# Differential heads joined ahead of one transpose and value product; latent heads scored in pairs

## What is computed

```
s = einsum('bqhmd,bkhmd->bhmqk', q, k) * scale + bias      # m = 0, 1: two score maps per head
p = softmax(s)
w = p[:, :, 0] - lam * p[:, :, 1]
o = einsum('bhqk,bkhd->bqhd', w, v)                        # one v for both maps
o = rms_norm(o, subln_g) * (1 - lam_init)
```

## Time and profile before

| | |
|---|---|
| median of 3 runs | 1736.49 us (1736.48 to 1736.52) |
| the profiled execution's own time | 1736.73 us |
| its span, first to last instruction | 1734.9 us |
| TensorE busy | 1584.0 us, 91% |
| VectorE, ScalarE, GpSimd busy | 938.1, 621.0, 218.0 us |
| mean granted TensorE clock | 0.96 of full |

### The profile page before, as it was taken

The page is one execution under the profiler, slowest core; times in us unless marked ns, Lnnn a source line. Parts: engine busy times, 40 slices in busy tenths (PEclk is TensorE's granted clock), DMA queues, the critical chain, the costliest instruction groups (busy, mean ns, idle before and its releaser), DMA issues.

```text
span 1734.9 us, 27116 instructions
## 1 busy us (share of the span) xinstructions
PE 1584.0 (91%) x10485; PEld 1216.5 (70%) x10485; DVE 938.1 (54%) x1543; ACT 621.0 (36%) x961; POOL 218.0 (13%) x241
## 2 busy tenths in 40 slices
PE   9999999777666677899999999999999999999998
PEld 6788985333223323688888888888888888888886
DVE  5675543111101111577786667777777767577767
ACT  5465441100010010433453653334433444553342
POOL 0232110000000000100015231000110114511000
PEclk9999999988889968999999999999999999999999
DMA  9515488999999999965545055533755445065501
GB/s 396 194 69 162 178 329 359 426 426 426 425 426 426 426 426 427 385 244 188 195 162 197 31 200 202 194 119 134 300 188 196 174 166 195 25 230 195 193 37 49
DMA packets 61100, 421.47 MB, mean 243 GB/s; under 512 B 7024, under 2 KB 16080, under 8 KB 17360
## 3 DMA queue, kind: packets, MB, share of 16 engines
q1 hardware_dynamic: 59280, 409.13, 60.0%
q10 hardware_dynamic: 1728, 11.03, 1.7%
HBM read 419.08 MB, written 1.05 MB: 242 GB/s over the span
## 4 chain that ended last, share of the span: by engine, by line
PE 69%; DMA 16%; SPq 6%; DVE 5%; ACT 2%; issue 2%; POOL 1%; DVEq 0%; ACTq 0%
PE bank L1168 17%; PE bank L1211 12%; DMA ring<-in_we 11%; PE bank L1170 9%; PE bank L2208 7%; SPq L2057 6%; PE bank L2137 5%; DMA more<-in_we 3%; PE bank L2372 2%; PE bank L2234 2%; PE bank L1551 2%; PE bank L2353 2%; PE bank L689 2%; DMA ring<-in_wf 2%; PE bank L1198 1%
## 5 line engine op out<-in xcount | busy, mean ns | idle before, releaser
L1168 PE MATMUL bank<-xhl,whu 128*128 128x512 f32 x1280 | 451.8, 396 | 0.0
L1170 PE MATMUL bank<-xhl,wlu 128*128 128x256 f32 x1280 | 357.5, 279 | 0.0
L1168 PEld LDWEIGHTS bank<-xhl,whu 128*128 128x128 f32 x1280 | 240.3, 188 | 57.8
L1170 PEld LDWEIGHTS bank<-xhl,wlu 128*128 128x128 f32 x1280 | 241.1, 188 | 3.3
L985 DVE TENSOR_TENSOR wlu<-ring,whu 128x2048 fp32r<-128x2048 f32 x84 | 192.5, 2292 | 43.8 <-ACT whu L980 43.8
L980 ACT ACTIVATE whu<-ring 128x2048 fp32r (+1 forms) x88 | 167.2, 1902 | 3.5 <-DMA ring<-in_wf 3.5
L985 DVE TENSOR_TENSOR wld<-ring,whd 128x1024 fp32r<-128x1024 f32 x80 | 98.6, 1233 | 113.3 <-ACT whd L980 113.3
L689 PE MATMUL bank<-ring,xg 128*32 128x256 f32 x1424 | 105.4, 436 | 38.1 <-DMA ring<-in_we 38.1
L980 ACT ACTIVATE whd<-ring 128x1024 fp32r (+1 forms) x80 | 84.8, 1060 | 128.5 <-PE bank L1211 128.5
L1278 ACT ACTIVATE sg<-sg 128x256 f32<-128x256 f32 x80 | 33.5, 418 | 265.8 <-DVE sg L1357 265.8
L2208 PE MATMUL bank<-ring_r,xTh 128*128 128x512 f32 x384 | 109.8, 397 | 4.6 <-DVE ring_r L520 2.5
(11 more groups left out here) (370 smaller groups left out, 2761.5 us busy)
## 6 DMA issues: line engine op xcount, KB each, us to landing
ring<-in_we SPq DMA_DIRECT2D x141, 1024.0 KB, 26.8
ring<-in_wf SPq DMA_DIRECT2D x88, 1536.0 KB, 6.5
ring<-in_w SPq DMA_DIRECT2D x52, 1024.0 KB, 5.1
more<-in_we SPq DMA_DIRECT2D x51, 1024.0 KB, 25.8
ring<-in_w SPq DMA_DIRECT2D x32, 256.0 KB, 3.7
ln<-in_ln ACTq DMA_DIRECT2D x6, 1024.0 KB, 6.0
bias<-in_bias ACTq DMA_DIRECT2D x2, 2048.0 KB, 9.4
bias<-in_bias SPq DMA_DIRECT2D x1, 2048.0 KB, 20.4
```

Of the source, the lines that this page charges most:

```text
L1168: pe.matmul(into[:].rearrange("p (a s) -> p a s", a=2), whu[p][:, cols], xhl[:, :, k], start=(k == 0), stop=False, skip_group_check=True)
L1170: ins = pe.matmul(into[:, 0:S], wlu[p][:, cols], xh[:, k], start=False, stop=(k == KD - 1), skip_group_check=True)
```

## The change

- The two score maps of a differential head are joined on VectorE as soon as both exponentials are there (`mix`): the second map, times minus lambda and the ratio of the two sums, is added to the first. The pair then has one transpose, one copy, one value product (`values2`: 16 in place of 20) and one output. The output of the value product before stands behind the join. The probabilities have a fourth buffer (`lg_d`, over the differential queries and keys).
- TensorE transposes a pair behind the scores of its second unit, and takes the values in the next unit.
- Latent queries and keys are laid out as the 64 plain columns of all heads and then the 32 rotated ones. Their transposes are three groups in place of four. A latent head's scores are two products (64 rows and 32 rows), and the heads are scored in pairs, the products of the two heads alternating (`AHEAD2`).
- Scores of units 14 and 15 no longer wait for the latent transposes (`QK_READY`). ScalarE's scaling of cat block 1 moves behind unit 18.
- In the first feed-forward pass ScalarE makes the high part of tile 1 behind the four casts of the activations. GpSimd makes half of its low part and VectorE the other half, and TensorE's `up(1, 1)` waits for these two alone.

```diff
+        lg_d = proj2[:, 0, D0:D0 + NT * S].rearrange("p (t s) -> p t s", t=NT)
...
-            q, _ = head_rows(qkT2, block2(10 + h), 0, BQ)
-            _, k = head_rows(qkT2, block2(14 + h), 0, BQ)
-            units2.append(Unit([q], [k], [vm[:, t, h, :] for t in range(NT)], 1.0,
+            qs = [head_rows(qkT2, block2(b), r, n)[0] for b, r, n in ((10 + h // 2, 64 * (h % 2), 64), (14, 32 * h, 32))]
+            ks = [head_rows(qkT2, block2(b), r, n)[1] for b, r, n in ((12 + h // 2, 64 * (h % 2), 64), (15, 32 * h, 32))]
+            units2.append(Unit(qs, ks, [vm[:, t, h, :] for t in range(NT)], 1.0,
...
         AHEAD2 = {0: (2, 3), 1: (4, 5), 3: (6, 7), 5: (8, 9), 7: (10, 11), 9: (12, 13), 11: (14, 15),
-                  **{u: (u + 4,) for u in range(12, 16)}}
+                  13: (16, 17), 15: (18, 19)}
...
+        values2 = [(n, n + 1) if unit.half == 0 else (n,) for n, unit in enumerate(units2) if unit.half != 1]
+        value_of = {n: v for v, heads in enumerate(values2) for n in heads}
+        PAIRS2 = sum(len(heads) == 2 for heads in values2)
+        VALUES2 = len(values2)
+        lg_buffers = [lg2[:, 0], lg2[:, 1], lg2_c[:], lg_d]
+        lg_at = [0, 1, 2, 0, *((n - 3) % 4 for n in range(4, UNITS2))]
+        lg_last = [max((m for m in range(n) if lg_at[m] == lg_at[n]), default=None) for n in range(UNITS2)]
+        lg_free = [0 if m is None else value_of[m] + 1 for m in lg_last]
...
+        def pool_second(pool, g, between=None, columns=range(0, 2 * D, 512)):
...
             pool.wait_ge(wh_ok, g * FFN_W + 2)
-            ffn_low_pieces(pool, 1, 1, pre_ok, between)
+            ffn_low_pieces(pool, 1, 1, pre_ok, between, columns)
...
+            def up(t, p, ready=None):
+                pe.wait_ge(*(ready or (wl_ok, t * 2 + (g * FFN_W + FFN_W + 1))))
...
-            up(1, 1)
+            up(1, 1, (pre_ok, 2) if g == 0 else None)
...
             if g == 0:
-                act_second(act, 0)
                 for j in range(4):
                     act.wait_ge(t_ps, tb + (j + 1))
                     act.activation(xh[:, 2 * j:2 * j + 2].rearrange("p k s -> p (k s)"), bank[4 + j][:], ACT.Copy)\
                        .then_inc(xh_ok, 1)
+                act_second(act, 0)
                 act_high_down(act, 0)
...
+            if g == 0:
+                dve.wait_ge(wh_ok, 2)
+                ffn_low_pieces(dve, 1, 1, pre_ok, columns=SECOND_HALF)
             dve.wait_ge(wh_ok, g * FFN_W + 3)
             ffn_low(dve, 0, 0, True, wl_ok)
-            dve.wait_ge(pre_ok, g + 1)
+            dve.wait_ge(pre_ok, g + 2)
             dve.memset(small[:, 234:235], 0.0).then_inc(wl_ok, 1)
...
-        QK_READY = {4: 7, 8: 10, 12: 11, 14: 15, 16: 15}
+        QK_READY = {4: 7, 8: 10, 12: 11, 16: 15}
...
-                    for k in range(2):
-                        ins = pe.matmul(bank[b][:, 0:BH * BQ], cT[:, k, tok(i)], slot[s][:, k * BH * BQ:(k + 1) * BH * BQ],
-                                        start=(k == 0), stop=(k == 1))
+                    for into, columns in ((slice(0, NOPE), slice(0, 64)), (slice(NOPE, BH * BQ), slice(64, BQ))):
+                        for k in range(2):
+                            w = slot[s][:, k * BH * BQ:(k + 1) * BH * BQ].rearrange("p (h d) -> p h d", h=BH)
+                            ins = pe.matmul(bank[b][:, into].rearrange("p (h d) -> p h d", h=BH), cT[:, k, tok(i)], w[:, :, columns],
+                                            start=(k == 0), stop=(k == 1))
                     ins.then_inc(mla_ps, 1)
...
-                    if 8 <= u < 12:
+                    if 8 <= u < 11:
                         j = u - 8
                         pe.wait_ge(t_out, tb + 11 + j)
                         for b in range(2):
                             for i in range(NT):
-                                ins = pe.transpose(bank[7][0:BQ, b * S + i * P:b * S + (i + 1) * P],
-                                                   (qm, km)[j % 2][:, i, 2 * (j // 2) + b], ident[:])
-                        ins.then_inc(t_ps, 1)
+                                part = (qm[:, i, b * P:(b + 1) * P], km[:, i, b * P:(b + 1) * P], (qm, km)[b][:, i, NOPE:])[j]
+                                ins = pe.transpose(bank[7][:, b * S + i * P:b * S + (i + 1) * P], part, ident[:])
+                        ins.then_inc(t_ps, (1, 1, 2)[j])
...
             for i in range(NT):
-                for unit in units:
-                    for b in range(len(unit.q)):
+                for b in range(len(units[0].q)):
+                    for unit in units:
                         ins = pe.matmul(bank[unit.bank][:, i * S:(i + 1) * S], unit.q[b][i], unit.k[b],
                                         start=(b == 0), stop=(b == len(unit.q) - 1))
-                    if i == NT - 1:
-                        ins.then_inc(sc_ps, 1)
+                        if i == NT - 1 and b == len(unit.q) - 1:
+                            ins.then_inc(sc_ps, 1)
...
+            def probs_T(v):
+                u = values2[v][0]
+                pe.wait_ge(pt_ok, v0 + v - 1)
+                if units[u].half is None:
+                    pe.wait_ge(ex_ok, n0 + u + 1)
+                else:
+                    pe.wait_ge(mix_ok, l * PAIRS2 + sum(len(heads) == 2 for heads in values2[:v + 1]))
+                lg = lg_buffers[lg_at[u]]
                 for t in range(NT):
                     for i in range(NT):
-                        ins = pe.transpose(bank[2 + u % 2][:, t * S + i * P:t * S + (i + 1) * P],
-                                           lg_ring[u % 3][:, i, t * P:(t + 1) * P], ident[:])
+                        ins = pe.transpose(bank[2 + v % 2][:, t * S + i * P:t * S + (i + 1) * P], lg[:, i, t * P:(t + 1) * P], ident[:])
                 ins.then_inc(pt_ps, 1)
+            def values(v):
+                unit = units[values2[v][0]]
+                pe.wait_ge(o_ok, v0 + v - 1)
+                pe.wait_ge(pt_ok, v0 + v + 1)
+                for i in range(NT):
+                    for t in range(NT):
+                        ins = pe.matmul(bank[4 + v % 2][:, i * unit.dv:(i + 1) * unit.dv], pT_at[:, v % 2, t, tok(i)], unit.v[t],
+                                        start=(t == 0), stop=(t == NT - 1))
+                ins.then_inc(pv_ps, 1)
...
+            for u, unit in enumerate(units):
+                v = value_of[u]
+                if unit.half is None:
+                    probs_T(v)
+                    if v >= 1:
+                        values(v - 1)
                 if u >= 1:
-                    values(u - 1)
                     between(u)
                     if u in AHEAD2:
                         scores(AHEAD2[u])
+                if unit.half == 0:
+                    values(v - 1)
+                elif unit.half == 1:
+                    probs_T(v)
             drain()
-            values(len(units) - 1)
...
             def exponentials(u):
-                unit, n, lg = units[u], n0 + u, lg_ring[u % 3]
-                act.wait_ge(lg_ok, n + 1)
-                act.wait_ge(o_ok, n - 3)
-                act.wait_ge(pt_ps, n - 2)
+                unit, lg = units[u], lg_buffers[lg_at[u]]
+                act.wait_ge(lg_ok, n0 + u + 1)
+                if u >= 4:
+                    act.wait_ge(o_ok, v0 + value_of[u - 4] + 1)
+                act.wait_ge(pt_ps, v0 + lg_free[u])
...
-            for u in range(len(units)):
-                n, b = n0 + u, u % 2
+            for u, unit in enumerate(units):
+                v = value_of[u]
                 if u + 1 < len(units):
                     exponentials(u + 1)
-                act.wait_ge(pt_ps, n + 1)
-                act.wait_ge(pv_ps, n - 1)
-                act.activation(pT_at[:, b].rearrange("p t s -> p (t s)"), bank[2 + b][:], ACT.Copy).then_inc(pt_ok, 1)
+                if unit.half != 0:
+                    act.wait_ge(pt_ps, v0 + v + 1)
+                    act.wait_ge(pv_ps, v0 + v - 1)
+                    act.activation(pT_at[:, v % 2].rearrange("p t s -> p (t s)"), bank[2 + v % 2][:], ACT.Copy).then_inc(pt_ok, 1)
                 behind(u)
                 between(u)
...
-                dve.wait_ge(pt_ps, n - 2)
+                dve.wait_ge(pt_ps, v0 + lg_free[u])
...
+            def mix(u, w):
+                dve.wait_ge(ex_ok, n0 + w + 1)
+                st.then(dve.reciprocal(rden4[:, u % 4], den4[:, u % 4]))
+                st.link(dve.reciprocal(rden4[:, w % 4], den4[:, w % 4]))
+                st.link(dve.scalar_tensor_tensor(nrd[:, 0], rden4[:, w % 4], nlam[:, 0:1], den4[:, u % 4], ALU.mult, ALU.mult))
+                first, second = (lg_buffers[lg_at[n]] for n in (u, w))
+                for i in range(NT):
+                    ins = dve.scalar_tensor_tensor(first[:, i, 0:S], second[:, i, 0:S], nrd[:, 0, i:i + 1], first[:, i, 0:S],
+                                                   ALU.mult, ALU.add)
+                ins.then_inc(mix_ok, 1)
...
+            def output(v):
```

(56 more changed lines are left out.)

78 lines of the change are left out of this document (27 added, 51 removed).

## The result

Five runs of the changed kernel took 1744.88, 1754.73, 1759.48, 1761.23 and 1761.79 us, against 1736.49 before. The medians lie 23 us apart; the ratio over all runs is 1.0117 with a 95% interval of [1.0098, 1.0137], which is 20 us. The forecast was 1737.7 with a range up to 1742.5. The profiled execution is the quickest of the five (1744.88, of it 1743.1 span).

A forecast was written before the change was run, and what follows sets the result against it. TensorE was taken as the bound, 91% busy, but the heads' new loop of waits would cost +2.0 us for both layers; with -0.8 for the first pass, +1.2 on 1736.7 gave 1737.9, forecast 1737.7, range 1729.0 to 1742.5.

The forecast's parts named there:

- the loop: Differential heads: copy, exponential, join, output and next exponential run in a chain, 4.2 us per pair whatever TensorE does.
- The join: VectorE, behind a pair's second exponential: reciprocals, small product and two multiply-adds, 1.3 us, bounds 1.0 and 1.6.
- the keys' product: TensorE, layer 0 heads: it waits until ScalarE, behind the first pair's copy, has evacuated the queries, 1.2 us idle.
- the exponential of head 16: Late in layer 0's heads: TensorE waits 0.4 us for it before scores 16 and 17's transposes and values are followed.
- scores 14 and 15 waiting over 2 us for ScalarE: Sign in the heads that the forecast is right: TensorE held there by exponential 12.
- rival (2): Slower: TensorE's granted clock falls around idle time in the heads; 2.3 us per layer gives 1742.3 us; chance 0.13.
- the latent pair: TensorE, scores of two latent heads: 16 passes take 2.12 us against 1.84, +0.56 us per layer; bounds 1.98 to 2.43.
- The first pass: First feed-forward pass: with casts first TensorE begins about 710.7, counted -0.8 us once; bounds -0.3 and -0.8.
- One sign that I had named as wrong: First feed-forward pass: TensorE waiting for GpSimd at tile 1 would show the forecast wrong.
- Rival (1): Heads: the loop is hidden and TensorE stays the bound, 1724.3 us, near 1731 in part; chance 0.21.

The follow-up runs named there:

- e1: The changed kernel again, nothing edited, to profile a usual run: 1755.68 us, ratio 1.0121 against the kernel before.
- e7: The kernel before with the latent edits alone (split query product, three transposes, paired scores), differential heads and first pass as before: 1737.12 us, ratio 1.0010.
- e11: The kernel before, with scores 14/15 no longer waiting for the last latent copies, nothing else: 1734.84 us, ratio 0.9993.
- e16: e7 with six GpSimd copies that TensorE waits for ahead of scores 14/15: 1756.24 us, ratio 1.0099 against the kernel before.
- e12: The kernel before, with TensorE waiting ahead of scores 14/15 for four added GpSimd copies: 1746.44 us, ratio 1.0063.
- e17: e6 with four GpSimd copies that TensorE waits for ahead of scores 14/15: 1748.26 us, ratio 1.0068 against the kernel before.
- e2: The kernel before with the edits of the first feed-forward pass alone: 1736.06 us, ratio 1.0002.
- e10: The kernel before with joins, exponential released by the join, earlier query copy, no wait of scores 14/15 for the last latent copies: 1729.23 us, ratio 0.9963.
- e4: The changed kernel with ten filler products of zeros in TensorE's wait ahead of scores 14/15: 1741.71 us, ratio 1.0038 against the kernel before.
- e5: The changed kernel with ScalarE's exponential slot released by the join, not the scaled output: 1737.19 us, ratio 1.0008 against the kernel before.
- e3: The changed kernel with the first feed-forward pass as before: 1759.32 us, ratio 1.0130 against the kernel before.
- e6: The kernel before with the joins alone, latent heads and first pass as before: 1740.01 us, ratio 1.0025.
- e8: e6 with the exponential's slot released by the join, not the scaled output: 1738.12 us, ratio 1.0020 against the kernel before.

## Why the prediction was wrong

**Right: the loop and its place.** That scores 14 and 15 wait for exponential 12 came as worked out: 8.4 us were forecast from the second pair's transposes to the end of that exponential; it was 8.7 (974.9 to 983.55). The join took 1.34 us (980.86 to 982.2; 1.3 forecast), the keys' product waited 1.07 (1.2), the exponential of head 16 0.29 (0.4). Scores 14/15 started at 983.70, where the schedule, moved by the 1.22 us carried in, has 983.4. So "scores 14 and 15 waiting over 2 us for ScalarE" was foreseen, and the wait was 2.68 us.

**Wrong: what a wait costs.** The step that failed is in rival (2): "Against it: the stretches of full clock in the heads, and that the idle pieces are short." The sum put the clock at nothing, and the rival had a chance of 0.13 and a price of 2.3 us a layer. But my own schedule left TensorE at work 4.65 of 8.4 us there, and my own signs had one of these pieces over 2 us long. In all eight profiles with a wait of 2.05 us or more at this place the clock fell, in both layers, in the wait or within 0.8 us of its end. In none of the seven with a wait of 1.41 us or less there did it fall behind that wait. In the quickest execution scores 14/15 to scores 16/17 took 6.56 us where 5.0 were forecast, about 1.6 us a layer and less than the rival's price. In a usual one (e1) the stretch from scores 6/7 on is 6.8 and 6.4 us longer still. Filling the wait brought 14 us back, and the wait alone cost the old kernel 10. The Trainium skill (TensorE: Matmul & The Clock Gate, What's actually happening) ties the clock to recent activity, and the runs agree (2.76 us of waiting: half clock; 1.41: full).

**Wrong by size: the latent pair.** Forecast 2.12 us, bounds to 2.43; measured 2.52 and 2.53 to the next instruction (from 990.26 and 996.29), above the bound: 0.4 us x 4 = 1.6 us. I had set a rule of the Trainium skill against my rows (TensorEngine Tiling (Array Packing), Key Properties: a change of the tiling mode drains the engine). The price that my rows gave it, 2.4, was the better estimate; no run here separates the drain from other costs of the smaller products. From scores 6/7 to the output products e7 takes 40.37 us and e11, which also gives up the wait of 0.78 us, 38.66: all latent edits together cost 1.7 us a layer at the full clock. At half clock the pair took 4.68 us and the clock stayed down.

**The latent edits were no free company.** I costed the parts one by one and added. Joins alone +3.9, latent edits alone +1.0, first pass 0, all together +20: what multiplies is a wait from the one part with the long half clock that the other brings (e16 against e12 and e17).

**The first pass.** It began without the wait: from the expert stage's last addition to the first gate's activation it is 9.22 us in place of 10.11 (708.82 to 718.04, before 707.25 to 717.36), the 0.8 forecast. That is partly luck: it hung on the one profile of before that I had. With the old pass the same stretch is 9.21 to 10.11 us in twelve profiles, 9.6 on average, and with the new one 9.21 or 9.22 in all seven, so the gain is some 0.4 us, too little to show in the time (1.0002). One sign that I had named as wrong is there as well: TensorE waits 0.26 us for GpSimd at tile 1 (718.26, and as much in e2), since GpSimd's half took 3.42 us and not 3.0. VectorE and GpSimd, side by side, each on its half, were both slower than expected (VectorE's timeline, GpSimd's, and VectorE's of the kernel before),

```profile
714.67 2.39 DVE L1004 TENSOR_TENSOR wlu<-ring,whu 128x512 fp32r<-128x512 f32 x2 [0.57 <-ACT whu L991]
716.99 2.30 DVE L996 TENSOR_TENSOR wld<-ring,whd 128x1024 fp32r<-128x1024 f32 x1
...
714.78 3.42 POOL L1004 TENSOR_TENSOR wlu<-ring,whu 128x512 fp32r<-128x512 f32 x2 [455.29 <-ACT whu L991]
...
713.70 1.89 DVE L985 TENSOR_TENSOR wld<-ring,whd 128x1024 fp32r<-128x1024 f32 x1
```

VectorE's two pieces of 128x512 took 2.39 us, where it splits a whole tile of 128x2048 in 2.28 while GpSimd is idle (709.43). Its next split took 2.30, where before it took 1.89, and 1.22 with GpSimd idle (720.34).

**Rival (1)** was closer than it looked. The loop is no bound of the work but of one semaphore: an output that held a slot which the join had already freed. With it, the query copy's place and the last latent wait mended, and the pairs left out, 6.3 us arrive (e10; 2 x 3.5 by its profile) of the 2 x (5.1 + 0.8) that the joins and that wait were to take off TensorE. Part of the rest is that the removed work was worth less: from scores 6/7 to output products TensorE's busy time fell from 38.06 to 34.07 us, by 4.0 and not 5.1. The other part is waits of 0.3 to 0.6 us: idle time there is 1.9 us, against 1.4 before with the wait of 0.78 in it.

## What to carry to other kernels

Price a wait of TensorE by what runs behind it as well: ask of each new wait whether it is longer than those that the trace shows at full clock, and if so, fill it with products of zeros, or cut it, before the change is judged by its time. No length was found to be safe: 1.41 us at one place did no harm, and 1.07 at another sometimes did. When parts are to be compared, measure a stretch that begins where the order of work is still the same in both kernels. Where runs of one kernel spread by 1% and those of the other by 0.1%, profile a usual run, not the quickest one. When work is merged, look for semaphores that stood for the work removed: the slot of an exponential was free at the join, one output earlier than the count said.

## What was not expected of the hardware

The same wait of 2.68 us was followed by 3.4 us at 1.2 GHz in one execution and by 17 in another; behind a wait of 2.84 us it was 27 us, in which TensorE was busy all the time. The paired scores (16 products on 64 and 32 rows) take 2.53 us, 4.68 at half clock, against 0.92 for one head's four products on 96 rows. Eight profiles have a wait of 1.07 us at the keys' product, in both layers. It was followed by half clock in layer 0 of e1 and e4 and in both layers of e5, and not in the other twelve cases (the first profile, e3, e6, e8, e17, and layer 1 of e1 and e4), so the length of one wait is not the whole of it.
